# The first modulation of a two-layer latent-token backbone: half of its sixteen weight units as split products, the norm of the first half among the input tiles, the loads in another order

## The chip, the cores and the metric

One NeuronCore of a Trainium2 chip runs the whole program. The metric is device microseconds of one execution; the engines are named as in the profile: PE (TensorE), DVE (VectorE), ACT (ScalarE), POOL (GpSimd), and SP, which issues most DMAs. The time before is the median of three runs.

## The reference

Two layers over 1024 latent tokens and 256 context tokens, width 1024, all in float32. What matters here stands at the very start of layer 0:

```
def adaln(cond, w, b):
    m = jax.nn.silu(cond) @ w + b          # w: 1024 x 6144, cut in six vectors of 1024
    return jnp.split(m[..., None, :], 6, axis=-1)

sh1, sc1, g1, sh2, sc2, g2 = adaln(c, mod_w[l], mod_b[l])
n_lat = modulate(rmsnorm(h, norm1_g[l]), sh1, sc1)
csh1, csc1, ... = adaln(c_ctx, mod_w[l], mod_b[l])
n_ctx = modulate(rmsnorm(hc, norm1_g[l]), csh1, csc1)
q, k, v, xr, gr = jnp.split(n_lat @ w_in, ...)      # and n_ctx @ w_in
```

The first projection can start once the shift and scale vectors (the first 2048 columns of `mod_w[0]`) and the normed tokens are there. Attention, a gated recurrence, a short-convolution layer and two SwiGLU feed-forwards follow; the change doesn't touch them.

## The kernel before

Everything is written out by hand: each engine has one block whose instructions run in the order in which they stand, and semaphores (`wait_ge`, `then_inc`) tie the engines together. Tokens lie transposed in SBUF, features on the 128 partitions.

Large products are made of a high and a low part. A float32 operand x becomes `hi`, x rounded to the fp32r format, and `lo` = x - hi; `product` runs three fp32r matmuls, w_hi·x_hi, w_lo·x_hi and w_hi·x_lo. The rounding is a copy (ACT, or a POOL multiplication with ones), the low part a subtraction (DVE or POOL).

The prologue, which is the stretch up to the first projection:

- ACT's queue loads ten tiles `x_in` of 128 tokens (eight latent, two context; 512 KB each). SP's queue loads small parameters, then sixteen modulation units of 512 KB, `load_first_mod(u)`, into the eight places of `mod_ring`; unit u holds rows 128k to 128k+127 and 1024 columns, with c = u // 8 telling shift from scale and k = u % 8. From unit 8 on a load waits until PE has used the unit eight before. Among them stand the loads `raw` of the first projection's weights (`load_unit`; two buffers).
- PE turns each tile (eight 128x128 transposes), DVE places it in `h_in`, ACT squares and sums it. After the last tile one square root, one reciprocal and ten diagonals `x_diag` follow on ACT and DVE; `x_spread(n)` on PE spreads 1/rms over the partitions, and DVE multiplies (`x_rms`, L2363, sixteen instructions of 128x512).
- `first_mod(u)` on PE (L1191) multiplies the unit by `cond` (two columns: the latent and the context condition) as plain float32 matmuls, 2 x 512 each, adding up in banks 4 to 7. ACT and DVE copy the sums to `mod_row`, `mod_turn` (L1206) turns them, DVE adds the bias (`mods`) and makes `gains`.
- Then the norm is finished, feature tile k by tile: `scaled` (DVE L2380 for even k, ACT for odd), `act_hi` (ACT L1825), `proj_lo` (DVE L2392). PE's `columns` waits for `proj_lo` of tile k (semaphore `norm_done`) before the three matmuls of that tile, L1102 to L1104. `GROUPS` sets PE's order: unit 0 on the first half of the tokens, unit 1 on the first half, both on the second half, and so on.
- Meanwhile POOL's `split(j, ...)` makes `w_hi` (L936) and `w_lo` (L939) of the first four projection units from `raw`, into four places `w_hi4`, `w_lo4`; the two `raw` buffers come free with the semaphore `unit_split`.

## Time and profile before

| | us |
|---|---|
| median of three runs | 2296.51 (2292.99 to 2296.66) |
| the profiled execution | 2295.41 |
| its span from first to last instruction | 2293.6 |
| PE busy in the span | 2234.5 |
| first projection matmul starts | 57.77 |

The profiled execution stands 1.1 us under the median, and 1.8 us of it lie outside the span. Times of rows are microseconds from the span's start. In a row of the timeline the first number is the start, the second the time to the end of the last of the instructions merged in it, and the bracket is the idle time ahead of it with what ended it. In a row of the windows each engine has its busy time and, in brackets, its instructions; behind them stand the granted TensorE clock (1.00 is 2.4 GHz, 0.50 is 1.2 GHz), the DMA engines' busy share and GB/s.

### The profile page before, as it was taken

Reading aid. Unit: us, or ns where it says so; the run is one execution under the profiler, and the core shown is the slowest. Engines: PE = TensorE matmul, PEld = TensorE weight load, DVE = VectorE, ACT = ScalarE, POOL = GpSimd, SP = SyncE. Lnnn points to the kernel's source line nnn. Section 1 sums busy time; section 2 is a strip of 40 time slices with the busy share of each in tenths; the row PEclk is TensorE's granted clock in tenths of the full one; section 3 lists DMA queues with packets and bytes.
Section 4 is the critical chain, followed back from the end, with each engine's and each line's share of the span. In section 5 each row is a group of like instructions: output and inputs, shape, how many; then the busy total and the mean of one; then the engine's idle time right before and its main releaser. Section 6 shows DMA issues by size and latency. Waiting matters only on the chain.

```text
span 2293.6 us, 27308 instructions
## 1 busy us (share of the span) xinstructions
PE 2234.5 (97%) x10246; PEld 1819.7 (79%) x10246; DVE 1480.8 (65%) x1897; ACT 841.0 (37%) x1396; POOL 1139.1 (50%) x726
## 2 busy tenths in 40 slices
PE   7999999999999999999999899999899999999998
PEld 3788887878778888888888678888688888888886
DVE  5677765854775555558777987665975555555553
ACT  3555546852533333332213522234533333332112
POOL 3222314788545555565443445574365555564340
PEclk9999999999999999999999999999999999999999
DMA  9756558734132222247652122260132222242321
GB/s 344 211 157 172 161 170 202 166 129 138 37 110 83 83 83 83 83 169 259 219 198 96 42 83 74 74 207 10 60 98 89 83 84 83 83 153 92 110 83 74
DMA packets 296942, 282.95 MB, mean 123 GB/s; under 512 B 64783, under 2 KB 242155, under 8 KB 296299
## 3 DMA queue, kind: packets, MB, share of 16 engines
q1 hardware_dynamic: 258747, 257.61, 36.3%
q10 hardware_dynamic: 37488, 21.50, 3.3%
q8 instruction: 82, 1.34, 0.2%
q0 software_dynamic: 576, 2.10, 0.2%
q14 instruction: 49, 0.40, 0.1%
HBM read 226.36 MB, written 57.16 MB: 124 GB/s over the span
## 4 chain that ended last, share of the span: by engine, by line
PE 70%; DVE 6%; POOL 1%; issue 1%; ACT 1%; DMA 1%; DVEq 0%; POOLq 0%; ACTq 0%
PE bank L1102 23%; PE bank L1104 23%; PE bank L1103 23%; DVE act_lo L2138 1%; DVE act_hi L2138 1%; DMA pair_raw<-in_o_w_in 1%; DVE x_rms L2130 0%; PE bank L1145 0%; DVE bank L2049 0%; DVE pair_raw L2115 0%; DVE low_f L2123 0%; POOL slot L1063 0%; PE bank L1129 0%; DVE t_sum L2105 0%; DVE a L2138 0%
## 5 line engine op out<-in xcount | busy, mean ns | idle before, releaser
L2057 DVE SCALAR_TENSOR_TENSOR h<-bank,mods,h 128x512 f32<-128x512 f32 x384 | 287.2, 750 | 260.8 <-PE bank L1104 255.6
L1063 POOL TENSOR_TENSOR slot_lo<-pair_raw,slot_hi 128x512 fp32r<-128x512 f32 x112 | 170.1, 1519 | 282.1 <-ACT slot_hi L1621 282.1
L1063 POOL TENSOR_TENSOR slot_lo<-t_sum,slot_hi 128x512 fp32r<-128x512 f32 x109 | 163.6, 1523 | 158.3 <-ACT slot_hi L1621 158.3
L1063 POOL TENSOR_TENSOR slot<-pair_raw,slot 128x512 fp32r<-128x512 f32 x144 | 233.8, 1644 | 16.0 <-ACT slot L1621 16.0
L2218 DVE TENSOR_TENSOR bank<-bank,p 128x512 f32<-128x512 f32 x53 | 37.0, 698 | 290.6 <-PE bank L1104 290.6
L1102 PE MATMUL bank<-act_lo,slot_hi 128*128 128x512 f32 x436 | 170.8, 392 | 6.6 <-DVE act_lo L2138 5.9
L1621 ACT CAST slot_hi<-pair_raw 128x512 fp32r<-128x512 f32 x112 | 69.0, 616 | 287.8 <-DMA pair_raw<-in_ffn_w_gu 239.1
L1102 PE MATMUL bank<-a,slot_hi 128*128 128x512 f32 x436 | 171.5, 393 | 2.3 <-ACT p L1630 0.8
L1104 PE MATMUL bank<-a,slot_hi 128*128 128x512 f32 x436 | 170.5, 391 | 0.0
L1104 PE MATMUL bank<-act_lo,slot_hi 128*128 128x512 f32 x436 | 169.8, 389 | 0.0
L1103 PE MATMUL bank<-a,slot_lo 128*128 128x512 f32 x436 | 169.7, 389 | 0.0
L1103 PE MATMUL bank<-act_lo,slot_lo 128*128 128x512 f32 x436 | 169.7, 389 | 0.0
L1102 PE MATMUL bank<-act_hi,w_hi 128*128 128x512 f32 x368 | 146.7, 399 | 3.3 <-DVE proj_lo L2392 2.7
L1103 PE MATMUL bank<-act_hi,w_lo 128*128 128x512 f32 x376 | 147.9, 393 | 0.0
L1074 POOL TENSOR_TENSOR act_lo<-low_f,act_lo 128x512 fp32r<-128x512 f32 x80 | 102.3, 1318 | 83.8 <-ACT act_lo L1661 83.8
L1103 PE MATMUL bank<-act_hi,slot 128*128 128x512 f32 x364 | 141.9, 390 | 0.0
L1104 PE MATMUL bank<-act_hi,slot 128*128 128x512 f32 x364 | 141.8, 390 | 0.0
L1102 PE MATMUL bank<-act_hi,slot 128*128 128x512 f32 x364 | 141.7, 389 | 0.0
L1621 ACT CAST slot_hi<-t_sum 128x512 fp32r<-128x512 f32 x109 | 67.8, 622 | 165.8 <-PE bank L1104 114.3
L1102 PE MATMUL bank<-act_lo 128*128 128x512 f32 x320 | 125.8, 393 | 0.0
L1104 PE MATMUL bank<-act_lo 128*128 128x512 f32 x320 | 125.1, 391 | 0.0
L1103 PE MATMUL bank<-act_lo 128*128 128x512 f32 x320 | 124.6, 389 | 0.0
(329 smaller groups left out, 5962.2 us busy)
## 6 DMA issues: line engine op xcount, KB each, us to landing
pair_raw<-in_ffn_w_gu SPq DMA_DIRECT2D x88, 512.0 KB, 4.4
mod_in_f<-in_mod_w SPq DMA_DIRECT2D x48, 512.0 KB, 3.7
z_spill<-silu_g SPq DMA_DIRECT2D x88, 256.0 KB, 2.7
mod_in_p<-in_mod_w SPq DMA_DIRECT2D x32, 512.0 KB, 4.7
pair_raw<-in_o_w_in SPq DMA_DIRECT2D x24, 512.0 KB, 3.7
raw<-in_e_w_in SPq DMA_DIRECT2D x20, 512.0 KB, 4.5
low_f<-z_spill SPq DMA_DIRECT2D x40, 256.0 KB, 5.0
a_f<-z_spill SPq DMA_DIRECT2D x18, 512.0 KB, 6.2
```

The lines of the kernel that those rows point to most:

```text
L1063: nc.gpsimd.tensor_tensor(low, from_, high, ALU.subtract).then_inc(s_wlo, 1)
L1074: nc.gpsimd.tensor_tensor(lo, full, hi, ALU.subtract).then_inc(s_l2, 1)
L1102: pe.matmul(dst, w_hi, x_hi, start=first, stop=False)
L1103: pe.matmul(dst, w_lo, x_hi, start=False, stop=False)
L1104: return pe.matmul(dst, w_hi, x_lo, start=False, stop=last)
L1621: nc.scalar.copy(slot(st, n, p)[0], from_).then_inc(s_whi, 1)
L2057: V.scalar_tensor_tensor(out=dst, in0=bank[:, b, :], scalar=mods[:, gate, m:m + 1], in1=dst, op0=ALU.mult, op1=ALU.add).then_inc(s_hup, 1)
L2138: V.tensor_tensor(lo, LOW_F[n][k], hi, ALU.subtract).then_inc(s_ld, 1)
L2218: V.tensor_tensor(to, bank[:, x_bank(p), :], p1_at(p), ALU.add).then_inc(s_made, 1)
```

## The change

- Eight of the sixteen units (`MOD_SPLIT`: 1, 3, 5, 7, 8, 10, 12, 13) become split products. ACT makes `mod_hi(u)` (rounding the unit, 128x1024), DVE `mod_lo(u)` = unit - hi (128x1024, both inputs in SBUF), and PE runs four fp32r matmuls with a stationary of four columns, the hi and the lo part of the two conditions (`cond_s`). The other eight stay float32, with two zero columns more (`cond_d`). The four rows of the sums are folded in `mod_turn`, now a float32 matmul with a 4x2 matrix of ones (`fold_rows`) and no transpose.
- `mod_hi` and `mod_lo` use places 2 and 3 of `w_hi4` and `w_lo4`. So POOL's `split(2)` waits until all sixteen units are summed.
- PE takes the units in another order, `MOD_ORDER`: 0, 2, 1, 4, 3, 6, 5, 7, 9, 8, 11, 10, 12, 14, 13, 15; five of them among the tiles.
- Square root, reciprocal and diagonals come in three parts (first four tiles, second four, context); the first half's `x_rms` stands among the last tiles on DVE, the second half's between four `mod_low`.
- Of the `raw` loads unit 0 comes behind modulation unit 11, units 1 to 3 behind all sixteen; before, units 0 and 1 came ahead of modulation unit 8, and 2 and 3 behind units 11 and 13.
- In the first projection PE waits for `act_hi` (semaphore `normed_hi`) ahead of the first two matmuls of a tile and for `proj_lo` only ahead of the third.

```diff
+        MOD_TILE = {4: (0,), 6: (2, 1), 8: (4, 3)}
+        MOD_ORDER = tuple(u for tt in sorted(MOD_TILE) for u in MOD_TILE[tt]) + (6, 5, 7, 9, 8, 11, 10, 12, 14, 13, 15)
+        MOD_SPLIT = (1, 3, 5, 7, 8, 10, 12, 13)
+        def mod_hi(u):
+            return w_hi4[:, 2 + MOD_SPLIT.index(u) % 2, :]
...
             def load_first_mod(u):
                 if u >= 8:
-                    sp.wait_ge(s_modmm, u - 7)
+                    sp.wait_ge(*mod_done(u - 8))
...
-            for j in range(2):
-                load_unit(j, j, column_unit(w_in, order_p[j]))
             for u in range(8, 2 * FT):
                 load_first_mod(u)
-                if u in (11, 13):
-                    j = (u - 7) // 2
-                    load_unit(j, j % 2, column_unit(w_in, order_p[j]))
+                if u == 11:
+                    load_unit(0, 0, column_unit(w_in, order_p[0]))
+            for j in range(1, 4):
+                load_unit(j, j % 2, column_unit(w_in, order_p[j]))
...
             for j in range(4):
+                if j == 2:
+                    pool.wait_ge(s_modmm, 2 * FT)
                 split(j, j, j % 2)
...
                 pe.matmul(dst, w_lo, x_hi, start=False, stop=False)
+                if low_at is not None:
+                    pe.wait_ge(*low_at)
                 return pe.matmul(dst, w_hi, x_lo, start=False, stop=last)
...
+                if u in MOD_SPLIT:
+                    pe.wait_ge(s_mhi, MOD_SPLIT.index(u) + 1)
+                    pe.wait_ge(s_mlo, MOD_DVE.index(u) + 2)
+                    for a in range(2):
+                        dst, half = bank[0:4, 4 + 2 * c + a, :], slice(a * HALF, (a + 1) * HALF)
+                        pe.matmul(dst, cond_s[:, k, :], mod_hi(u)[:, half], start=first, stop=False)
+                        mm = pe.matmul(dst, cond_s[:, k, :], mod_lo(u)[:, half], start=False, stop=last)
...
-                    mm = pe.transpose(bank[:, 3, 2 * (c * FT + m):2 * (c * FT + m) + 2], mod_row[:, c, m * P:(m + 1) * P],
-                                      ident[0:2, 0:2])
+                    mm = pe.matmul(bank[:, 3, 2 * (c * FT + m):2 * (c * FT + m) + 2], mod_row[:, c, m * P:(m + 1) * P],
+                                   fold_rows[:], start=True, stop=True)
...
+            def mod_high(u):
+                n = MOD_SPLIT.index(u)
+                act.wait_ge(s_mod[u % 8], 16 * (u // 8 + 1))
+                if n >= 2:
+                    act.wait_ge(*mod_done(MOD_SPLIT[n - 2]))
+                nc.scalar.copy(mod_hi(u), mod_ring[:, u % 8, :]).then_inc(s_mhi, 1)
...
+            def mod_low(j):
+                u = MOD_DVE[j]
+                dve.wait_ge(s_mhi, MOD_SPLIT.index(u) + 1)
+                V.tensor_tensor(mod_lo(u), mod_ring[:, u % 8, :], mod_hi(u), ALU.subtract).then_inc(s_mlo, 1)
```

What the change moves on two engines, before and after. DVE, from the last context tile to the last modulation vector, before (`x_rms` is the multiplication by the spread 1/rms, `mods` the vectors with their bias):

```order
L2350 COPY ctx_t<-bank 128x8x128 [waits x_turned] x2
L2352 RECIPROCAL x_std<-x_std 128x10 [waits x_rms_ready]
L2355 TENSOR_SCALAR sp_t<-par 128x8 [waits par_placed]
L2356 TENSOR_TENSOR sp_t<-sp_t,par 128x8 [waits dve_step]
L2357 TENSOR_SCALAR half_b<-par 128x16
L2363 TENSOR_TENSOR x_rms<-h_in,bank 128x512 [waits rstd_spread,dve_step]
L2363 TENSOR_TENSOR x_rms<-h_in,bank 128x512 [waits dve_step] x7
L2363 TENSOR_TENSOR x_rms<-h_in,bank 128x512 [waits rstd_spread,dve_step]
L2363 TENSOR_TENSOR x_rms<-h_in,bank 128x512 [waits dve_step] x7
L2336 TENSOR_TENSOR mods<-bank,mod_bias 128x8 [waits mod_turned]
```

And the same place after, from the first context tile on, where the low parts of units 5, 7 and 8 are the rows that end in `mod_unit_hi` waits:

```order
L2449 COPY ctx_t<-bank 128x8x128 [waits x_turned]
L2429 TENSOR_TENSOR x_rms<-h_in,bank 128x512 [waits rstd_spread]
L2429 TENSOR_TENSOR x_rms<-h_in,bank 128x512 [waits dve_step] x3
L2449 COPY ctx_t<-bank 128x8x128 [waits dve_step,x_turned]
L2434 TENSOR_TENSOR w_lo<-mod_ring,w_hi 128x1024 [waits mod_unit_hi]
L2423 RECIPROCAL x_std<-x_std 128x2 [waits x_rms_ready]
L2434 TENSOR_TENSOR w_lo<-mod_ring,w_hi 128x1024 [waits mod_unit_hi]
L2465 TENSOR_SCALAR sp_t<-par 128x8 [waits par_placed]
L2466 TENSOR_TENSOR sp_t<-sp_t,par 128x8 [waits dve_step]
L2467 TENSOR_SCALAR half_b<-par 128x16
L2429 TENSOR_TENSOR x_rms<-h_in,bank 128x512 [waits rstd_spread,dve_step]
L2429 TENSOR_TENSOR x_rms<-h_in,bank 128x512 [waits dve_step]
```

Eight subtractions of 128x1024 have come in on DVE, two of them ahead of this piece and the last four each behind two of the second half's `x_rms`.

POOL, the four splits of the first projection's weights, before:

```order
L936 TENSOR_TENSOR w_hi<-raw,ones 128x1024 [waits raw_landed0,ident_made]
L939 TENSOR_TENSOR w_lo<-raw,w_hi 128x1024 [waits unit_hi]
L936 TENSOR_TENSOR w_hi<-raw,ones 128x1024 [waits raw_landed1]
L939 TENSOR_TENSOR w_lo<-raw,w_hi 128x1024 [waits unit_hi]
L936 TENSOR_TENSOR w_hi<-raw,ones 128x1024 [waits raw_landed0]
L939 TENSOR_TENSOR w_lo<-raw,w_hi 128x1024 [waits unit_hi]
L936 TENSOR_TENSOR w_hi<-raw,ones 128x1024 [waits raw_landed1]
L939 TENSOR_TENSOR w_lo<-raw,w_hi 128x1024 [waits unit_hi]
L952 MEMSET gate_w 128x512 [waits norm_done,h_spilled]
```

And after:

```order
L958 TENSOR_TENSOR w_hi<-raw,ones 128x1024 [waits raw_landed0,ident_made]
L961 TENSOR_TENSOR w_lo<-raw,w_hi 128x1024 [waits unit_hi]
L958 TENSOR_TENSOR w_hi<-raw,ones 128x1024 [waits raw_landed1]
L961 TENSOR_TENSOR w_lo<-raw,w_hi 128x1024 [waits unit_hi]
L958 TENSOR_TENSOR w_hi<-raw,ones 128x1024 [waits raw_landed0,mod_summed]
L961 TENSOR_TENSOR w_lo<-raw,w_hi 128x1024 [waits unit_hi]
L958 TENSOR_TENSOR w_hi<-raw,ones 128x1024 [waits raw_landed1]
L961 TENSOR_TENSOR w_lo<-raw,w_hi 128x1024 [waits unit_hi]
L976 MEMSET gate_w 128x512 [waits norm_done,h_spilled]
```

The instructions are the same; the third split now also waits for `mod_summed`, the end of PE's last modulation unit.

## Rows read from the trace of the kernel before

**Rows 1.** The page, part 1: busy time of each engine

```profile
PE 2234.5 (97%) x10246; PEld 1819.7 (79%) x10246; DVE 1480.8 (65%) x1897; ACT 841.0 (37%) x1396; POOL 1139.1 (50%) x726
```

**Rows 2.** Timeline of PE, 31 to 66 us

```profile
31.18 8.74 PE L1191 MATMUL bank<-mod_ring,cond 128*2 128x512 f32 x20
...
48.31 5.31 PE L1191 MATMUL bank<-mod_ring,cond 128*2 128x512 f32 x12
54.43 0.62 PE L1206 MATMUL bank<-ident,mod_row 2*128 2x2 f32 x8 [0.82 <-ACT mod_row L1803]
57.77 0.77 PE L1102 MATMUL bank<-act_hi,w_hi 128*128 128x512 f32 x1 [2.71 <-DVE proj_lo L2392]
...
65.34 0.39 PE L1103 MATMUL bank<-act_hi,w_lo 128*128 128x512 f32 x1
65.57 0.39 PE L1104 MATMUL bank<-proj_lo,w_hi 128*128 128x512 f32 x1
```

**Rows 3.** Windows of the prologue and the first projection

```profile
15.40:18.80 3.40, 3.30 (x4) 0.37 (x4) 0.00 (x0) 1.95 (x4) 0.00 (x0) 0.53 1.03 410
...
53.60:57.70 4.10, 0.64 (x9) 0.57 (x8) 2.85 (x8) 1.96 (x4) 0.00 (x0) 0.81 1.18 456
57.70:62.90 5.20, 5.13 (x12) 3.85 (x13) 4.46 (x8) 5.14 (x9) 0.00 (x0) 0.50 0.98 417
62.90:104.00 41.10, 41.10 (x205) 34.87 (x205) 32.75 (x61) 20.13 (x35) 11.52 (x10) 1.00 0.78 217
104.00:112.00 8.00, 7.10 (x33) 5.67 (x32) 2.25 (x3) 5.43 (x8) 2.74 (x2) 1.00 0.65 122
```

**Rows 4.** Timeline of DVE, 22 to 58 us

```profile
22.80 1.23 DVE L2350 COPY h_in<-bank 128x1024 f32<-128x1024 f32 x1 [1.60 <-PE bank L1221]
...
33.44 1.81 DVE L2356 TENSOR_TENSOR sp_t<-sp_t,par 128x8 f32<-128x8 f32 x1
...
41.13 11.52 DVE L2363 TENSOR_TENSOR x_rms<-h_in,bank 128x512 f32<-128x512 f32 x16 [5.79 <-PE bank L1197]
...
53.66 0.68 DVE L2367 COPY mod_row<-bank 2x512 f32<-2x512 f32 x1 [0.73 <-PE bank L1191]
...
55.37 0.17 DVE L2082 SCALAR_TENSOR_TENSOR gains<-mods,par 128x8 f32<-128x8 f32 x1
...
55.65 1.00 DVE L2380 TENSOR_SCALAR scaled<-x_rms,gains,mods 128x512 f32<-128x512 f32 x2
56.93 0.69 DVE L2392 TENSOR_TENSOR proj_lo<-scaled,act_hi 128x512 fp32r<-128x512 f32 x1 [0.28 <-ACT act_hi L1825]
```

**Rows 5.** Timeline of POOL, 33 to 48 us

```profile
33.34 1.90 POOL L936 TENSOR_TENSOR w_hi<-raw,ones 128x1024 fp32r<-128x1024 f32 x1
...
45.37 2.35 POOL L939 TENSOR_TENSOR w_lo<-raw,w_hi 128x1024 fp32r<-128x1024 f32 x1
```

**Rows 6.** Timeline of DVE, 86 to 111 us

```profile
86.79 2.50 DVE L2437 SCALAR_TENSOR_TENSOR x_conv<-x_pad,par,x_conv 128x256 f32<-128x256 f32 x1
89.22 3.42 DVE L2437 SCALAR_TENSOR_TENSOR x_conv<-x_pad,par,x_conv 128x1024 f32<-128x1024 f32 x1
...
109.35 1.22 DVE L2487 TENSOR_TENSOR xc_lo<-x_conv,xc_hi 128x1024 fp32r<-128x1024 f32 x1
```

**Rows 7.** Timeline of POOL, 86 to 92 us

```profile
86.54 2.48 POOL L939 TENSOR_TENSOR w_lo<-raw,w_hi 128x1024 fp32r<-128x1024 f32 x1 [1.77 <-ACT w_hi L1857]
88.97 2.59 POOL L939 TENSOR_TENSOR w_lo<-raw,w_hi 128x1024 fp32r<-128x1024 f32 x1
```

**Rows 8.** Timeline of ACT, 85 to 88 us

```profile
85.41 2.00 ACT L1857 CAST w_hi<-raw 128x1024 fp32r<-128x1024 f32 x2
```

**Rows 9.** The matmuls of line L1145, 290 to 1100 us (min/median/max ns)

```profile
L1145 PE MATMUL bank<-ones,mod_acc_p x16: 165/250/250, 342.2 to 343.8; 128*128 128x1 f32 x16
```

**Rows 10.** Waits of SP's queue, first 200 us: total, times, longest

```profile
SPq L658 <- POOL gate_w L952: 7.3, 1, 7.3
```

**Rows 11.** Window of the first 48 us

```profile
0.00:48.00 48.00, 39.46 (x161) 17.22 (x162) 21.86 (x26) 20.12 (x40) 18.99 (x22) 0.96 0.95 342
```

More of the change, by code:

```diff
@@ L922, in _ @@
             nc.gpsimd.memset(ones[:], 1.0).then_inc(s_ident, 1)
+            steps.run(nc.gpsimd.memset(cond_d[:, :, 2:4], 0.0))
+            nc.gpsimd.tensor_tensor(fold_rows[:], ident[0:4, 0:2], ident[0:4, 2:4], ALU.add).then_inc(s_ident, 1)
             nc.gpsimd.memset(far_rows[:], FAR).then_inc(s_far, 1)
@@ L1098, in _, with product @@
         def _(pe):
-            def product(dst, w, x_hi, x_lo, first, last):
+            def product(dst, w, x_hi, x_lo, first, last, low_at=None):
                 w_hi, w_lo = w
@@ L1188, in first_mod @@
                 c, k = divmod(u, FT)
-                pe.wait_ge(s_mod[u % 8], 16 * (u // 8 + 1))
-                for a in range(2):
-                    mm = pe.matmul(bank[0:2, 4 + 2 * c + a, :], cond[:, k, :], mod_ring[:, u % 8, a * HALF:(a + 1) * HALF],
-                                   start=(k == 0), stop=(k == FT - 1))
+                nth = sum(v // FT == c for v in MOD_ORDER[:MOD_ORDER.index(u)])
+                first, last = nth == 0, nth == FT - 1
+                if u in MOD_SPLIT:
[5 more added lines that the diff above has]
+                        mm = pe.matmul(dst, cond_s[:, k, :], mod_lo(u)[:, half], start=False, stop=last)
+                else:
+                    pe.wait_ge(s_mod[u % 8], 16 * (u // 8 + 1))
+                    for a in range(2):
+                        mm = pe.matmul(bank[0:4, 4 + 2 * c + a, :], cond_d[:, k, :], mod_ring[:, u % 8, a * HALF:(a + 1) * HALF],
+                                       start=first, stop=last)
                 mm.then_inc(s_modmm, 1)
             def x_spread(n):
+                pe.wait_ge(s_rstd, n + 1)
                 for j in range(NORMS[n][2] // P):
@@ L1780, in _, with x_root, x_diagonals, mod_rows @@
             nc.scalar.activation(x_std[:, 1, 0:1], zero[:, 0:1], ACT.Silu).then_inc(s_xsq, 1)
+            def x_root(n):
+                lo, hi = tiles_of(n)
+                act.wait_ge(s_xsq, hi + 1)
+                nc.scalar.activation(x_std[:, 1, lo:hi], x_std[:, 0, lo:hi], ACT.Sqrt, bias=eps_t[:, 0:1], scale=1.0 / D).then_inc(s_xstd, 1)
+            def x_diagonals(n):
+                lo, hi = tiles_of(n)
+                act.wait_ge(s_xinv, n + 1)
+                act.wait_ge(s_turn, 2)
+                for j in range(lo, hi):
+                    last = nc.scalar.activation(x_diag[:, j, :], ident[:], ACT.Copy, scale=x_std[:, 2, j:j + 1])
+                last.then_inc(s_rstd, 1)
+            def mod_high(u):
[4 more added lines that the diff above has]
+                nc.scalar.copy(mod_hi(u), mod_ring[:, u % 8, :]).then_inc(s_mhi, 1)
+            def mod_rows(c):
+                act.wait_ge(s_modmm, FT * (c + 1))
+                for a in range(2 - c):
+                    nc.scalar.copy(mod_row[:, c, a * HALF:(a + 1) * HALF], bank[0:4, 4 + 2 * c + a, :]).then_inc(s_modrow, 1)
+            HIGH_AT = {5: (1,), 7: (3,), 9: (5, 7)}
             for tt in range(TT + CT):
@@ L2339, in _, with x_inverse, x_normed @@
                 dve.sem_inc(s, credits)
+            def x_inverse(n):
+                lo, hi = tiles_of(n)
+                dve.wait_ge(s_xstd, n + 1)
+                V.reciprocal(x_std[:, 2, lo:hi], x_std[:, 1, lo:hi]).then_inc(s_xinv, 1)
+            def x_normed(n, fs):
+                dve.wait_ge(s_bc, n + 1)
+                for f in fs:
+                    src, _, w, *_ = NORMS[n]
+                    steps.run(V.tensor_tensor(x_rms[:, f, cols(n)], src[:, f, cols(n)], bank[:, SPREAD[n], 0:w], ALU.mult))
+            def mod_low(j):
+                u = MOD_DVE[j]
+                dve.wait_ge(s_mhi, MOD_SPLIT.index(u) + 1)
+                V.tensor_tensor(mod_lo(u), mod_ring[:, u % 8, :], mod_hi(u), ALU.subtract).then_inc(s_mlo, 1)
+            LOW_AT = {6: 0, 7: 1}
             for tt in range(TT + CT):
+                if tt == 5:
+                    x_inverse(0)
+                if tt == TT:
+                    x_inverse(1)
                 if tt == 4:
@@ L2357, in _ @@
             steps.run(V.tensor_scalar(half_b[:], par[:, PAR["br"]:PAR["br"] + 16], 0.5, None, ALU.mult))
-            for n in (0, 1):
-                dve.wait_ge(s_bc, n + 1)
-                for f in range(FT):
-                    src, _, w, *_ = NORMS[n]
-                    steps.run(V.tensor_tensor(x_rms[:, f, cols(n)], src[:, f, cols(n)], bank[:, SPREAD[n], 0:w], ALU.mult))
-                if n == 1:
-                    mod_first(0)
+            for q in range(4):
+                x_normed(1, range(2 * q, 2 * q + 2))
+                mod_low(4 + q)
+            mod_first(0)
             dve.wait_ge(s_modmm, 2 * FT)
-            V.tensor_copy(mod_row[:, 1, HALF:UNIT], bank[0:2, 7, :]).then_inc(s_modrow_d, 1)
+            V.tensor_copy(mod_row[:, 1, HALF:UNIT], bank[0:4, 7, :]).then_inc(s_modrow_d, 1)
             mod_first(1)
```

110 lines of the change are left out of this document (74 added, 36 removed).

## The prediction

> **What bounds the kernel now.** The page's busy times come first: PE works in 97% of the span [rows 1], so whatever moves the start of its dense part moves the end. The timeline of PE then shows where the dense part starts: modulation units without a pause from 31.18 to 39.9 and, behind the spreads, three more units from 48.31 to 53.62, the turn of the last sums from 54.43, and the first projection matmul at 57.77, which waited 2.71 us for `proj_lo` [rows 2]. The windows show what follows: 41.10 of 41.10 us busy from 62.9 to 104, and 0.90 us idle in the next 8 [rows 3]. So nothing behind the prologue has slack worth naming, and I carry a shift of the first projection to the end one to one. The same windows show the clock: 0.53 in 15.4 to 18.8 and 0.50 in 57.7 to 62.9, each behind a gap of PE, and 1.00 from 62.9 on [rows 3].
>
> I take two marks. T is the end of the last modulation unit, 53.6. H is the end of unit 0 on the first half of the tokens, 65.8: the last of its 24 matmuls starts at 65.57 and they follow each other by 0.23 [rows 2]. H - T is 12.2.
>
> **PE's own work.** A float32 unit takes 1.77 us (three in 5.31), a split one four matmuls at 0.23, 0.92 [rows 2]. Eight times 0.85 is 6.8 us less for PE. If PE were all that counts, T would be 46.8. The turn becomes eight float32 matmuls instead of eight transposes: at most the 1.7 us of the sixteen records of L1145 [rows 9], at least the 0.62 of the transposes [rows 2]; I take 1.3, near the former, since the form is the same (eight float32 matmuls with few columns). Its second use stands behind T.
>
> **DVE's work.** It gets eight subtractions of 128x1024 with both inputs in SBUF. The same form took 1.22 us for `xc_lo` [rows 6]: 9.8 us. ACT's eight roundings at 1.0 [rows 8] are lighter, but its queue stops once: the diagonals of tiles 4 to 7 wait for a reciprocal that DVE makes only behind four `x_rms`, at about 32, so unit 5 is rounded at 35.5 and unit 7 at 37.
>
> I follow the queues. Unit 0 is unchanged and cold (to 18.8 [rows 3]). Tile 5, the first spread and tile 6 bring PE to 21.9; DVE places tile 6 (1.23 [rows 4]) until 23.1 and makes low 1 until 24.4; PE has unit 1 until 25.3 and tile 7 until 26.4; DVE places it until 27.6. From there DVE has seven subtractions (8.5), sixteen `x_rms` (11.52 [rows 4]), two placements (2.5) and small things (0.9): 23.4 us in one queue, so 51.0 without a single wait. PE meanwhile is through with unit 6 at 32.9, and needs low 5, which stands behind eight `x_rms` and both context placements and ends at 38.5 at best. That is an idle of 5.6 us or more, and as behind the gaps of [rows 3] I expect the clock at 0.50 behind it, for some 5 us: units 5 and 7 and the second spread at half speed. The second half's `x_rms` wait for that spread, which costs DVE 1 to 2 us.
>
> **What POOL does to DVE.** This is the term on which the sign hangs. When POOL ran `w_lo` from 86.54 to 89.02, DVE's 128x256 operation issued at 86.79 ended at 89.29, and the 128x1024 one behind it took 3.42, until 1.1 us after POOL's second `w_lo` ended at 91.56 [rows 6, 7]. At 33.44 even an operation on 128x8 took 1.81, until POOL's `w_hi` ended at 35.24 [rows 4, 5]. Against that, sixteen `x_rms` (one input in SBUF, one in PSUM) took 0.72 each [rows 4] though POOL worked until 47.7 [rows 5]. So I read: DVE operations that take all from SBUF and POOL's take turns, each waiting for the whole of the other; those with an input in PSUM don't. All eight `mod_low`, `gains`, `scaled` and `proj_lo` are of the first kind. The Trainium skill, page "SBUF — State Buffer", section "Who interferes with whom", says the same: a VectorE instruction with two SBUF inputs, or in a two-port mode, fully blocks against a GpSimd one that reads SBUF. By that rule the sum is the one below; by a reading without it, it would be +0.5 to +4.3 (the first rival). The page speaks against this change.
>
> The loads put the clashes in place. The DMA engines moved 342 GB/s over the first 48 us at 0.95 busy [rows 11]. `raw` of unit 0 is now the 23rd piece of 0.524 MB, 12.1 MB, so it lands at 35 to 36. POOL splits it in two pieces of 1.90 and 2.35 [rows 5], just when DVE comes to low 5 and low 7: low 5 waits 0.9, low 7 2.2. Units 13 to 15 wait for PE's units 5 to 7 and `raw` 1 stands behind them, landing at 48 to 50; its split costs low 12 and low 13 another 0.5 to 2.7. Together: 51.0, plus 1 to 2 for the spread, plus 3.5 to 4.5, is about 56; unit 13 (0.9) and unit 15 (1.8) behind the last low part give **T = 58.8**, between 57.7 and 60.2. That is +5.2, although PE has 6.8 us less to do.
>
> **Behind T.** Before: POOL was idle from 47.7 [rows 5], `gains` at 55.37, `scaled` at 55.65, the first `proj_lo` from 56.93 to 57.62 [rows 4], that is T + 4.0. Now `split(2)` and `split(3)` start at T: 1.90, 2.35, 1.90, 2.35, together 8.5. DVE's `mod_row` copy and `mods` read PSUM and pass; two `gains` and the first `scaled` get one turn each between POOL's pieces, and they lengthen POOL's row by 0.7. The first `proj_lo` ends at about T + 10.1, 6.1 later than before, whether the turn takes 0.7 or 1.3. The changed wait lets PE start with the high part some 0.9 us ahead of that, which before would have been worth 0.85; now it only fills time for which PE is late anyway. From there `proj_lo` comes at 0.95 per tile as before, and PE ends unit 0 at T + 18.2: **H - T = 18.2 instead of 12.2, +6.0**. Bounds: +3.5 if POOL starts late enough that one of its pieces falls behind the first `scaled`, +8 if the first `scaled` loses a further turn.
>
> **At no cost.** The loads of units 4 and 5 and the sixteen bias fills on SP's queue, which now wait for `split(2)` and `split(3)`; behind them stand the gate weights, for which SP waited 7.3 us for POOL's memset anyway [rows 10], and that memset follows `norm_done`, so moves by the same shift. The gate matmuls are 45 us further. If the fills were not through, gates would be late by one to three us. The spilling of `h_in` goes with T.
>
> **Sum.** 5.2 + 6.0 = 11.2 on the profiled execution's 2295.4 is 2306.6; with the median 1.1 above it the same sum gives 2307.7. I forecast **2307**.
>
> **Rivals.**
> - *No turns between POOL and DVE for these forms.* For it: `x_rms` was untouched [rows 4], and no row shows a subtraction of 128x1024 caught. Then T is 54.1 with PE warm behind its gap and 57.9 with the clock at 0.50, and H - T stays at 12.2: +0.5 to +4.3, so 2296 to 2300. 11 in 100, mostly inside the bound of no change.
> - *Part of the clashes.* POOL's splits of units 0 and 1 fall beside DVE's `x_rms`, and only those behind T count, or the other way: +5 to +8.5, 2300.5 to 2304. 15 in 100.
> - *Faster.* DVE is not in PE's way: `mod_low` and `x_rms` run at less than the 1.22 and 0.72 of the rows, or the early part of PE's queue is not held by low 5. It decides if DVE's 23.4 us shrink below 15: then PE's 6.8 and the 0.85 of the wait come through, less 0.7 for the turn: 2288.5. Against it stand two rows of [rows 4, 6]. 6 in 100.
> - *More than the forecast.* PE stays at clock 0.50 through units 9 to 15, since it starts and stops: four float32 units at 3.4 instead of 1.77 add 6.5, less the slack of 3 us in which it waits: +15 and more, 2311 to 2316. 8 in 100.
> - The forecast itself, +9 to +14: 60 in 100.
>
> **Range and chances.** 2299 to 2313 takes the forecast, the partly paid case and the cold edge, and leaves the faster case, most of the first rival and the far cold end outside. About 0.2%, 4.6 us, is what a measurement of this kernel can tell from no change. Faster 0.06, the same 0.10, slower 0.84.
>
> **What the changed profile would show.** PE idle for 5 us or more ahead of the split unit 5, which waits for DVE. The clock under 1.00 in the windows of 38 to 45. Subtractions of 128x1024 on DVE with a mean near 1.7 us where single ones take 1.2. T at 58 to 60. Behind T four POOL operations in a row, `gains` and the first `scaled` each ending when one of POOL's ends, and the first projection matmul at T + 8 to T + 10. From 80 us on the same rows as before, shifted. I am wrong if low parts take 1.2 beside POOL, or if T lies below 53, or if the shift of the first projection does not reach the end.

## The result and the profile after

| | before | after |
|---|---|---|
| median | 2295.8 us (2292.99 to 2296.66, 6 runs) | 2310.49 us (2307.62 to 2311.86, 6 runs) |
| profiled execution | 2295.41 | 2311.86 |
| its span | 2293.6 | 2310.1 |

The ratio is 1.006, with an interval from 1.0049 to 1.007, which is 11 to 16 us; by the medians the changed kernel is 14.7 us slower. The forecast was 2307, from 2299 to 2313.

PE's busy time has hardly moved from 2234.5 [rows 1]:

```profile
PE 2237.3 (97%) x10262; PEld 1828.3 (79%) x10262; DVE 1491.8 (65%) x1908; ACT 849.3 (37%) x1408; POOL 1140.5 (49%) x728
```

The timeline of PE, which answers to [rows 2]: the start, the time to the end, and in brackets the idle time ahead of the row with what ended it.

```profile
30.89 1.88 PE L1228 MATMUL bank<-mod_ring,cond_d 128*4 128x512 f32 x4
39.17 0.58 PE L1223 MATMUL bank<-w_hi,cond_s 128*4 128x512 f32 x1 [6.41 <-DVE w_lo L2434]
39.56 0.63 PE L1224 MATMUL bank<-w_lo,cond_s 128*4 128x512 f32 x1
...
49.90 1.94 PE L1244 MATMUL bank<-fold_rows,mod_row 4*128 4x2 f32 x16
...
56.17 1.88 PE L1228 MATMUL bank<-mod_ring,cond_d 128*4 128x512 f32 x4
58.87 1.91 PE L1244 MATMUL bank<-fold_rows,mod_row 4*128 4x2 f32 x16 [0.82 <-ACT mod_row L1846]
65.43 0.77 PE L1126 MATMUL bank<-act_hi,w_hi 128*128 128x512 f32 x1 [4.65 <-ACT act_hi L1903]
67.74 0.80 PE L1130 MATMUL bank<-proj_lo,w_hi 128*128 128x512 f32 x1 [1.12 <-DVE proj_lo L2499]
...
74.30 0.39 PE L1130 MATMUL bank<-proj_lo,w_hi 128*128 128x512 f32 x1
```

PE has unit 6 done at 32.8 and stands for 6.41 us until DVE's low part of unit 5 is there. From 39.17 on it has no pause until the last modulation unit ends, T = 58.05, which is 4.4 later than before. The turn takes 1.91 where the transposes took 0.62 [rows 2]. The first projection matmul waits for `act_hi` and starts at 65.43, 7.7 later than before, and unit 0 on the first half, whose last matmul starts at 74.30, ends at H = 74.5, 8.7 later. So H - T is 16.5, where it was 12.2.

DVE's timeline, which answers to [rows 4]:

```profile
36.89 2.14 DVE L2434 TENSOR_TENSOR w_lo<-mod_ring,w_hi 128x1024 fp32r<-128x1024 f32 x1
38.95 0.15 DVE L2423 RECIPROCAL x_std<-x_std 128x2 f32<-128x2 f32 x1
39.03 3.31 DVE L2434 TENSOR_TENSOR w_lo<-mod_ring,w_hi 128x1024 fp32r<-128x1024 f32 x1
...
44.30 1.23 DVE L2434 TENSOR_TENSOR w_lo<-mod_ring,w_hi 128x1024 fp32r<-128x1024 f32 x1
...
61.09 1.37 DVE L2160 SCALAR_TENSOR_TENSOR gains<-mods,par 128x8 f32<-128x8 f32 x1
...
62.58 4.51 DVE L2487 TENSOR_SCALAR scaled<-x_rms,gains,mods 128x512 f32<-128x512 f32 x2
67.01 1.28 DVE L2499 TENSOR_TENSOR proj_lo<-scaled,act_hi 128x512 fp32r<-128x512 f32 x2
```

And POOL's, which answers to [rows 5]:

```profile
36.05 1.89 POOL L958 TENSOR_TENSOR w_hi<-raw,ones 128x1024 fp32r<-128x1024 f32 x1 [22.11 <-DMA raw<-in_e_w_in]
38.03 3.23 POOL L961 TENSOR_TENSOR w_lo<-raw,w_hi 128x1024 fp32r<-128x1024 f32 x1
50.07 2.37 POOL L958 TENSOR_TENSOR w_hi<-raw,ones 128x1024 fp32r<-128x1024 f32 x1 [8.81 <-DMA raw<-in_e_w_in]
...
58.13 1.89 POOL L958 TENSOR_TENSOR w_hi<-raw,ones 128x1024 fp32r<-128x1024 f32 x1 [2.40 <-PE bank L1228]
60.10 2.34 POOL L961 TENSOR_TENSOR w_lo<-raw,w_hi 128x1024 fp32r<-128x1024 f32 x1
62.40 1.90 POOL L958 TENSOR_TENSOR w_hi<-raw,ones 128x1024 fp32r<-128x1024 f32 x1
64.37 2.43 POOL L961 TENSOR_TENSOR w_lo<-raw,w_hi 128x1024 fp32r<-128x1024 f32 x1
```

The two are to be laid side by side. Low 5 ends at 39.03, 1.1 behind the end of POOL's `w_hi` at 37.94; low 7 ends at 42.34, 1.1 behind the end of `w_lo` at 41.26; where POOL is idle a low part takes 1.23. `gains`, eight columns wide, ends at 62.46, as POOL's piece ends at 62.44. Two `scaled`, which took 1.00 together before [rows 4], take 4.51: each stands for one POOL piece.

The windows, which answer to [rows 3]:

```profile
34.00:46.00 12.00, 6.83 (x20) 3.03 (x20) 11.53 (x14) 5.49 (x10) 5.12 (x2) 0.72 0.52 164
...
66.00:70.00 4.00, 2.88 (x7) 1.83 (x6) 3.96 (x6) 3.47 (x7) 0.80 (x1) 0.50 0.91 278
84.00:118.00 34.00, 34.00 (x174) 29.06 (x174) 20.84 (x40) 10.45 (x20) 12.40 (x11) 1.00 0.73 173
118.00:130.00 12.00, 8.70 (x37) 6.45 (x36) 3.75 (x4) 11.41 (x18) 5.24 (x3) 0.86 0.27 63
```

Behind the pause of 6.41 the granted clock is at its lower level for a while (0.72 over 34 to 46). The first projection is dense again (34.00 of 34.00 us busy), and the gates that follow it, idle for 0.90 of 8 us before [rows 3], now leave PE 3.3 of 12 us.

That is not all. Take each matmul's start, matched from the last matmul backwards, and subtract the start of the same matmul before: the difference is the **shift**, and it shows where the profiled execution loses what. The columns are places, in microseconds of the kernel before:

```
 66 (H)   104    130    340    400    455    500   1290   1400    end
  8.7     8.7   11.2   12.3   13.5   13.9   15.2   15.2   16.3   16.5
```

Only 8.7 of the 16.5 us arise in the prologue. The other 7.7 come later: 2.5 at the gates, 1.1 until 340, 1.1 around 372, where attention loads `k_lo`, 1.3 around 464, and 1.1 around 1350. The two profiled executions do not stand at their medians: of the 16.5, 1.8 are theirs (2311.86 is 1.4 above its median, 2295.41 is 0.4 below). The kernel before, run 70 times more on three chips, took from 2293.1 to 2299.7, so a single step of 1 to 2 us in such a row need not belong to the kernel.

### The profile page after: what moved, and what is told of

It reads as the page before. It is cut to its first block, busy times and chain, and to the rows that moved or that the text cites. A ratio compares the mean times of both kernels' runs of the same rounds, so it can differ in the third digit from the quotient of the medians.

```text
span 2310.1 us, 27370 instructions
## 1 busy us (share of the span) xinstructions
PE 2237.3 (97%) x10262; PEld 1828.3 (79%) x10262; DVE 1491.8 (65%) x1908; ACT 849.3 (37%) x1408; POOL 1140.5 (49%) x728
## 4 chain that ended last, share of the span: by engine, by line
PE 71%; DVE 5%; issue 1%; ACT 1%; POOL 1%; DMA 0%; DVEq 0%; POOLq 0%; ACTq 0%
PE bank L1126 23%; PE bank L1130 23%; PE bank L1127 23%; DVE act_lo L2216 1%; DVE act_hi L2216 1%; DVE x_rms L2208 0%; PE bank L1172 0%; DVE bank L2127 0%; DVE low_f L2201 0%; DVE pair_raw L2193 0%; PE bank L1156 0%; DVE a L2216 0%; PE bank L1374 0%; DVE x_rms L2210 0%; PE bank L1195 0%
```

## Experiments

Each run is given with its median against that of the kernel before on the same chip (2296.4, 2296.6 and 2296.8 in the three groups), its T and H - T, and later its shifts in one table. The ratio with its interval is not exactly the quotient of the two medians; the difference in us is that of the medians.

**POOL's late splits alone** (in the kernel before):

```diff
             for j in range(4):
+                if j == 2:
+                    pool.wait_ge(s_modmm, 2 * FT)
                 split(j, j, j % 2)
```

> The kernel before, with one line of the change: POOL's third and fourth split wait until all sixteen modulation units are summed. Everything else, the loads too, stays as before. If POOL and DVE take turns, the four POOL operations (8.5 us) run from T = 53.6 to 62 beside gains, scaled and proj_lo: the first scaled pair ends 3 to 5 us later, the first projection matmul moves from 57.8 to 62 or 64, unit 0 on the first half ends 4 to 6 us later, and the end comes 4 to 8 us later. If they don't take turns, nothing on PE moves and the time is within 1 us of before.

Measured: 2302.09, ratio 1.0023 (1.0014 to 1.0032), +5.7. T is 52.2, H 69.0: H - T is 16.9 instead of 12.2, as much as the changed kernel shows behind T (16.5). T itself lies 1.4 earlier than before; that is the clock at unit 0, told at the run on the turn. DVE's timeline:

```profile
54.29 4.60 DVE L2382 TENSOR_SCALAR scaled<-x_rms,gains,mods 128x512 f32<-128x512 f32 x2
58.81 3.43 DVE L2394 TENSOR_TENSOR proj_lo<-scaled,act_hi 128x512 fp32r<-128x512 f32 x2
```

POOL's four pieces start at 52.27 and end at 61.08. So one added wait, with nothing else changed, costs 4.7 us on the path.

**The split wait alone** (in the kernel before):

```diff
                 pe.matmul(dst, w_lo, x_hi, start=False, stop=False)
+                if low_at is not None:
+                    pe.wait_ge(*low_at)
                 return pe.matmul(dst, w_hi, x_lo, start=False, stop=last)
...
-                        pe.wait_ge(s_norm, 8 * norm + k + 1)
+                        pe.wait_ge(s_nhi, 8 * norm + k + 1)
...
```

> The kernel before, with the split wait alone: in the first projection PE waits for act_hi ahead of the first two matmuls of a tile and for proj_lo ahead of the third. I expect the first projection matmul at 57.0 instead of 57.8 and the end 0.5 to 0.9 us earlier, which the timing can hardly tell from nothing. The rival: PE only starts and stops more often, at clock 0.50 for longer, and nothing or up to 2 us is lost.

Measured: 2300.59, ratio 1.0011 (1.0003 to 1.002), +4.2. PE begins the projection 0.7 earlier and ends unit 0 0.4 earlier, as expected; and still the kernel is slower, by more than the rival's 2 us if one takes the medians (the ratio's interval is 0.7 to 4.6 us). In the profiled execution the shift says where: 0.4 at 340 and 4.9 at 400. PE's timeline there:

```profile
375.52 0.80 PE L1315 MATMUL bank<-k_hi,q_st 128*128 128x512 f32 x1 [3.85 <-DMA k_lo<-k_spill]
376.12 0.63 PE L1316 MATMUL bank<-k_lo,q_st 128*128 128x512 f32 x1
```

The same two matmuls in the kernel before:

```profile
372.54 0.50 PE L1312 MATMUL bank<-k_hi,q_st 128*128 128x512 f32 x1 [1.41 <-DMA k_lo<-k_spill]
372.88 0.40 PE L1313 MATMUL bank<-k_lo,q_st 128*128 128x512 f32 x1
```

The data came 3.0 later, though nothing that makes `k_lo` was touched: SP issued the load 0.9 later (363.54 against 362.64), and it took 11.9 us to land instead of 9.9. Behind the longer pause the matmuls run at half the clock (0.63 for 0.40). This execution, at 2302.59, was the slowest of the kernel's twelve; two others took 2295.35 and 2296.16, no more than the kernel before. So the loss at `k_lo` is shown for one execution, and the same kernel may do without it.

**The splits held until both halves are normed** (in the changed kernel):

```diff
                 if j == 2:
                     pool.wait_ge(s_modmm, 2 * FT)
+                    pool.wait_ge(s_norm, 2 * FT)
```

> The changed kernel, with POOL's third split waiting further, until DVE has finished the norms of both halves (norm_done 16), so that no POOL operation runs beside gains, scaled and proj_lo. If the turns cost what the trace after shows behind T (16.5 from T to the end of unit 0 on the first half, against 12.2), the stretch falls back to 11.5 to 12.5 and the end comes 4 to 5 us earlier than with the change, near 2306. The rival: the later splits of units 2 and 3 and the loads, bias fills and gate weights behind them on SP's queue come too late, and PE waits ahead of its sixth group or ahead of the gates; then the gain is eaten, 2310 or more.

Measured: 2315.18, ratio 1.0079 (1.0067 to 1.0091), +18.8. The local gain is there: T 57.3, H 70.0, so H - T is 12.7 instead of 16.5. It is more than lost further on. What waits for the late splits is late (the loads of units 4 and 5, the bias fills, the gate weights, for which ACT waited 3.13), and at the gates the shift goes from 5.4 to 16.1. This is what the rival had said. ACT and PE there:

```profile
123.82 1.04 ACT L1936 CAST w_hi<-raw 128x1024 fp32r<-128x1024 f32 x1 [6.95 <-DMA raw<-in_e_w_in]
```

```profile
128.62 0.58 PE L1127 MATMUL bank<-xc_hi,gate_hi 128*128 128x256 f32 x1 [6.74 <-ACT lru_r L1987]
```

**No split units** (in the changed kernel; norm among the tiles, order of units, order of loads, float32 turn and split wait stay):

```diff
-        MOD_SPLIT = (1, 3, 5, 7, 8, 10, 12, 13)
+        MOD_SPLIT = ()
...
-                if j == 2:
-                    pool.wait_ge(s_modmm, 2 * FT)
                 split(j, j, j % 2)
...
```

> The changed kernel without its split products: all sixteen units float32 with four columns, no rounding on ACT, no subtraction on DVE, no waiting of POOL for the sums; the order of units, the norm of the first half among the tiles, the order of the loads and the turn as matmuls stay. If the eight subtractions and their place behind x_rms on DVE are what keeps T at 58, T comes back to 52.5 to 54.5 and the end to 2293 to 2297. The rival: the order of DVE (x_rms ahead of the context tiles, late raw loads) is to blame by itself, and T stays at 56 or more.

Measured: 2300.82, ratio 1.0018 (1.001 to 1.0027), +4.4. PE:

```profile
47.87 7.03 PE L1226 MATMUL bank<-mod_ring,cond_d 128*4 128x512 f32 x16
...
59.62 0.77 PE L1124 MATMUL bank<-act_hi,w_hi 128*128 128x512 f32 x1 [1.99 <-ACT act_hi L1900]
```

T is 54.9, 3.1 earlier than with the eight split units, and H - T 12.7. The parts that save PE work cost 3.1 us ahead of T and, by their wait on POOL, 3.8 behind it. T and the time lie somewhat above what was expected (54.5, and 2297 at most); the rival, T at 56 or more, is out.

**DVE's queue in another order** (in the changed kernel):

```diff
-            LOW_AT = {6: 0, 7: 1}
+            LOW_AT = {6: 0, 7: 1, 8: 2, 9: 3}
...
-                if tt == TT:
+                if tt == TT - 1:
                     x_inverse(1)
+                    x_normed(0, range(0, 2))
...
+            x_normed(0, range(2, FT))
+            dve.sem_inc(s_xr, 1)
+            mod_low(4)
...
```

> The changed kernel with DVE's queue in another order: the reciprocal of tiles 4 to 7 and two x_rms ahead of the placement of tile 7, the low parts of units 5 and 7 right behind the context placements, the other six x_rms of the first half behind them. Nothing is left out. Theory (PE's idle of 6.41 us ahead of unit 5 is the order's, since ACT's rounding stood 7.46 us behind a reciprocal that DVE made late): unit 5 follows unit 6 within 1 us, PE waits 2 to 4 us ahead of unit 9 instead, the last unit ends at 52 to 54 instead of 58.05, the rest as in the changed kernel: 2304.5 to 2307. Rival (DVE's total of low parts and x_rms, 23 us in one queue, sets the end whatever the order): the last unit ends at 57 or later, 2309 to 2311.

Measured: 2307.72, ratio 1.0045 (1.0031 to 1.0059), +11.1. The time lies between the two claims. The pause ahead of unit 5 is gone (it starts at 32.06 instead of 39.17), but T is 59.2, 1.1 later than in the changed kernel, where the rival had it (57 or later). PE's timeline:

```profile
45.22 0.39 PE L1223 MATMUL bank<-w_hi,cond_s 128*4 128x512 f32 x1 [3.39 <-DVE w_lo L2434]
...
46.48 3.57 PE L1244 MATMUL bank<-fold_rows,mod_row 4*128 4x2 f32 x16
```

and DVE's:

```profile
38.29 2.34 DVE L2463 TENSOR_SCALAR sp_t<-par 128x8 f32<-128x8 f32 x1
...
42.40 2.67 DVE L2434 TENSOR_TENSOR w_lo<-mod_ring,w_hi 128x1024 fp32r<-128x1024 f32 x1
```

The early units brought the load of `raw` for unit 1 forward, POOL's second split began at 42.10 instead of 50.07, and it fell on low 10. An operation on 128x8 took 2.34, until POOL's `w_lo` ended at 40.60. From 45.9, behind the pause of 3.39, PE was at half clock until 56, the first turn among it with 3.57.

**The same with POOL silent up to T:**

```diff
-                if j == 2:
+                if j == 0:
                     pool.wait_ge(s_modmm, 2 * FT)
```

> The kernel with DVE's queue in the other order (a_order), and POOL holds all four splits of the first projection's weights, not only the third and fourth, until the last modulation unit is summed. Nothing is left out; behind that unit it must be slow, only the prologue up to there is looked at. Theory (in a_order POOL's splits of units 0 and 1 took turns with low 10, low 12 and a constant, 1.4 + 0.7 + 2.2 us, and the pause before low 10 put the granted clock at 0.50 for the next ten us): all low parts take 1.22, PE has no pause over 3 us, the last modulation unit ends at 52 to 54.5 instead of 59.1. Rival (DVE's total sets the end): 57 or later with low parts at 1.22. The time: 2312 to 2320.

Measured, in a single execution: 2307.8, less than the 2312 to 2320 expected. DVE's low 10, and PE's last unit:

```profile
39.17 1.22 DVE L2434 TENSOR_TENSOR w_lo<-mod_ring,w_hi 128x1024 fp32r<-128x1024 f32 x1
```

```profile
49.61 1.88 PE L1228 MATMUL bank<-mod_ring,cond_d 128*4 128x512 f32 x4
```

Every low part takes 1.22 to 1.23 and T is 51.5: 7.7 earlier, and 2.1 earlier than in the kernel before. Not all of it is POOL's silence: unit 0 took 1.88 here and 3.39 in the run before this one, and unit 9 started 1.05 earlier (36.07 against 37.12) although no low part had met POOL by then. Of the 2.1 against the kernel before, where unit 0 took 3.41, some 1 is left by the same estimate. So the split units cost nothing, and seem to gain a little, if DVE is left alone and its queue is in a fitting order. What POOL still had to do then came behind T (H - T 17.6), and the shift grew to 9.8 by the gates.

**The form of the turn** (in the kernel before):

```diff
-                    mm = pe.transpose(bank[:, 3, ...], mod_row[:, c, m * P:(m + 1) * P], ident[0:2, 0:2])
+                    mm = pe.matmul(bank[:, 3, ...], mod_row[:, c, m * P:(m + 1) * P], ident[0:2, 0:2], start=True, stop=True)
```

> The kernel before with the turn of the modulation rows as eight float32 matmuls by a 2x2 identity instead of eight transposes. Nothing is left out. Theory (the turn's form costs 1.3 us each time, 1.9 instead of 0.62, and both stand on PE's path): turn 1.9 us, the first projection 2.6 us later than 57.77 if the first turn is on the path too, 1.3 if it hides in PE's waits: 2297.7 to 2299. Rival (it is the four rows, not the form): turn below 1 us, no change in the prologue, and what differs in time is from later phases.

Measured: 2301.2, ratio 1.002 (1.0011 to 1.003), +4.6.

```profile
53.58 1.91 PE L1206 MATMUL bank<-ident,mod_row 2*128 2x2 f32 x16 [0.82 <-ACT mod_row L1803]
```

With two rows it takes 1.91 too: it is the form (sixteen records for eight instructions), not the four rows. H comes 0.9 later. T was 52.8 here, 0.9 earlier than before although the first turn was 1.3 longer. The trace shows why: unit 0 started 0.6 earlier (14.88) and took 1.88 where it had taken 3.41. This is the kernel before, and under it the run with POOL's late splits, whose program is the same up to there:

```profile
15.50 3.41 PE L1191 MATMUL bank<-mod_ring,cond 128*2 128x512 f32 x4 [2.79 <-DMA mod_ring<-in_mod_w]
```

```profile
15.59 1.88 PE L1193 MATMUL bank<-mod_ring,cond 128*2 128x512 f32 x4 [2.80 <-DMA mod_ring<-in_mod_w]
```

The pauses are equal and the clock behind them is not. The four matmuls of unit 0 took 1.88 in four of the fourteen profiled executions and 2.30 to 3.57 in the others, behind pauses of 2.4 to 2.8, and that difference of the clock moves T and H by some 1.5 us with no change in the program. So where T or H of two kernels differ by less than 1.5 us, one execution of each doesn't tell them apart; H - T is free of what happens at unit 0. The rest of the 4.6 comes later.

**A version meant to keep the gain.** Units 1, 3, 5 and 7 alone are split; POOL, idle then, makes the low parts; they lie in places of input tiles that are through, so `split(2)` waits for nothing; two `raw` loads and two `x_rms` stand earlier; the turn is a transpose of four rows:

```diff
+        mod_h = [at(40, "mod_h0", [P, UNIT], F32R), at(48, "mod_h1", [P, UNIT], F32R)]
+        mod_l = [at(44, "mod_l0", [P, UNIT], F32R), at(52, "mod_l1", [P, UNIT], F32R)]
...
+            for n, u in enumerate(MOD_SPLIT):
+                pool.wait_ge(s_mhi, n + 1)
+                nc.gpsimd.tensor_tensor(mod_lo(u), mod_ring[:, u % 8, :], mod_hi(u), ALU.subtract).then_inc(s_mlo, 1)
             for j in range(4):
-                if j == 2:
-                    pool.wait_ge(s_modmm, 2 * FT)
                 split(j, j, j % 2)
...
```

> A version meant to keep what the split units give and to drop what they cost: only units 1, 3, 5 and 7 are split, their low parts are made by POOL (idle until raw lands) and not by DVE, high and low parts lie in places of input tiles that are through, so that POOL's third split waits for nothing and raw of units 0 and 1 are loaded behind modulation units 10 and 12; the turn is a transpose of four rows again and DVE adds the pairs. Nothing is left out. Theory: PE has no idle behind unit 6, 4 x 0.85 us less than with sixteen float32 units, so the last unit ends at 51 to 52, and the end of unit 0 on the first half follows by 12.3 (POOL's splits are through): at 63.5 to 64.5, 1.3 to 2.3 us earlier than before; if nothing is lost later, 2294 to 2295. Rival 1 (POOL's splits reach beyond the last modulation unit, so DVE takes turns with them again): the distance is 15 us or more, 2298 or later. Rival 2 (later phases lose 2 to 4 us in any kernel whose prologue moves, as in the four runs so far): 2297 to 2299.

Measured: 2297.89 (2297.02 to 2300.57), ratio 1.0006 (0.9997 to 1.0015): no difference from the kernel before, as the second rival had it (2297 to 2299). PE's timeline:

```profile
43.80 7.03 PE L1232 MATMUL bank<-mod_ring,cond_d 128*4 128x512 f32 x16
51.65 0.62 PE L1248 MATMUL bank<-ident,mod_row 4*128 4x4 f32 x8 [0.82 <-ACT mod_row L1851]
54.66 0.77 PE L1130 MATMUL bank<-act_hi,w_hi 128*128 128x512 f32 x1 [2.38 <-ACT act_hi L1904]
```

The prologue is what it was to be, and better: T 50.8, H 62.7, both about 3 us earlier than before, with unit 0 as slow as there (3.46 against 3.41). Its profiled execution, 2.7 above its own median, was 5.2 later at the end: 2.4 were lost until 340 and 4.9 around the load of `k_lo`.

**Only a later start.** POOL clears a buffer four times or twice ahead of every load, and nothing else changes:

```diff
+            for _ in range(4):
+                steps.run(nc.gpsimd.memset(raw[:, :, :], 0.0))
+            pool.sem_inc(s_go, 2)
...
+            sp.wait_ge(s_go, 1)
...
+            act.wait_ge(s_go, 1)
```

Four times, in the kernel before:

> The kernel before with nothing changed but a start that is some 8 to 12 us late: POOL clears a buffer four times before the first load of any queue is issued. Nothing is left out. Theory 1 (what is lost behind the prologue in the changed kernels, 6 to 8 us in the profiled runs, comes from the order of events, above all from loads and buffers that move against PE): here all moves together, the shift of PE against before is the same at 60, 372, 465, 1303 and at the end within 0.7 us, and the time is 2296.4 plus the delay. Theory 2 (the granted clock falls behind the same short gaps of PE at some times of the execution and not at others): the shift grows by 1.5 to 3 us at 465 or 1303 with a granted clock under 1.00 there, though nothing moved against anything.

Twice, in the kernel before, in the changed kernel and in the last version:

> The kernel before with POOL clearing the buffer twice ahead of all loads: the start is 3.7 us late and nothing else changed. With four clearings the start was 7.5 us late and the median rose by 9.2. Theory 1 (the kernel before stands at a favourable place, and any other place loses 1 to 3 us behind the prologue, at 372, 465, 620 and 1350): 3.7 + 1 to 3, 2301 to 2303.5. Theory 2 (what is lost grows with the delay): 3.7 + 0.8, 2301. Theory 3 (chance of the runs): anything between 2298 and 2305, not the same as either.

> The changed kernel with POOL clearing the buffer twice ahead of all loads, 3.7 us late. If the loss behind the prologue (some 5.5 us of the changed kernel's 14) belongs to its order of events, it stays: 2313.5 to 2315. If it depends on where in time the later pauses fall, it can shrink or grow: 2311 to 2317, and the shift of PE against the changed kernel is not 3.7 throughout.

> The version with four split units and low parts on POOL (a_best: the first projection 3.2 us earlier than before, the end 1.3 us later by the medians), 3.7 us late by two clearings. Its prologue then ends 0.5 us behind that of the kernel before. If what it lost later (8 us in the profiled run) is the price of arriving earlier, against loads that don't come earlier, the shift at 372 us is the same as there and the time is 2298 to 2299. If the loss belongs to the version itself, it is 2301 to 2302.

| | start of PE later by | median against before | ratio |
|---|---|---|---|
| before, four clearings | 7.5 | +9.2 (2305.82) | 1.0038 (1.0025 to 1.005) |
| before, two | 3.6 | +5.4 (2302.18) | 1.0022 (1.0013 to 1.0031) |
| the changed kernel, two | 3.4 | +14.7 (2311.51) | 1.0062 (1.005 to 1.0075) |
| the last version, two | 3.6 | +4.9 (2301.66) | 1.0022 (1.0013 to 1.0031) |

By the medians either delay of the kernel before loses 1.7 to 1.8 more than itself, which is what the first theory said; but the intervals (6 to 11 us and 3.0 to 7.1 us) contain the bare delays of 7.5 and 3.6, so that the extra is not shown. The changed kernel with two clearings has the ratio of the changed kernel without (1.006), and its median is 1.0 higher (2311.51 against 2310.49): most of the 3.4 us at the start do not come out at the end, though the intervals leave room for about 3 us either way. The last version lost the 3.6 (2301.66 against 2297.89), which fits a loss that is its own and not only the price of an earlier arrival.

The shifts of all profiled executions against the kernel before, at the same places as above:

```
                         66(H)   104   130   340   400   455   500  1290  1400   end
changed kernel             8.7   8.7  11.2  12.3  13.5  13.9  15.2  15.2  16.3  16.5
POOL's late splits         3.2   3.2   3.0   3.5   3.5   5.8   5.9   5.8   5.5   5.5
split wait                -0.4  -0.4  -0.1   0.4   4.9   4.9   6.4   6.6   7.2   7.1
held until normed          4.2   5.4  16.1  17.3  19.1  19.5  20.8  20.8  20.0  20.2
no split units             1.8   1.8   3.1   3.2   3.5   3.6   4.9   4.9   5.2   5.3
DVE's other order         10.2  10.2  11.1  12.0  12.7  13.1  14.3  14.2  14.6  14.8
... and POOL silent        3.3   6.1   9.8  10.2  10.6  11.1  12.4  12.4  12.2  12.4
float32 turn               0.9   0.9   0.5   1.4   3.5   3.5   4.8   4.8   6.1   6.1
last version              -3.1  -3.1  -1.6  -0.7   4.2   4.2   4.4   4.1   5.2   5.2
before, 7.5 later          7.9   7.9   8.5   8.6   8.4   8.4   8.5   8.3   9.4   9.4
before, 3.6 later          4.6   4.6   5.0   5.1   5.6   5.7   6.8   6.8   7.1   7.1
changed, 3.4 later        12.6  12.6  14.4  14.8  14.9  15.3  16.4  16.4  16.0  16.1
last version, 3.6 later    0.2   0.2   1.5   1.7   4.5   4.5   6.2   6.0   6.3   6.3
```

Two things stand out in the medians and the columns. Every kernel's median is above what its own prologue (the column H) gave, by 0.8 to 6.0 us, and by 14.6 in the kernel held until both halves are normed; so something is lost behind the prologue in all of them. At which places it is lost is seen in one execution of each only. Between 340 and 400 the kernels that come to the load of `k_lo` at +1.7 or less lose 2.1 to 4.9, those that come later -0.2 to 1.8; the kernel before, at 0, waited 1.41 and kept its clock. And between 455 and 500 all but three lose 1.1 to 1.7. There the windows of 6.7 us from the same matmul on, behind a pause of 2.3 us in each, read in the kernel before, with two and with four clearings:

```profile
463.30:470.00 6.70, 6.59 (x42) 5.60 (x43) 5.66 (x12) 6.29 (x13) 5.68 (x4) 1.00 0.01 4
```

```profile
469.00:475.70 6.70, 6.66 (x37) 6.05 (x38) 4.76 (x11) 5.12 (x11) 5.71 (x4) 0.78 0.01 3
```

```profile
471.70:478.40 6.70, 6.59 (x42) 5.60 (x43) 5.66 (x12) 6.28 (x13) 5.69 (x4) 1.00 0.04 14
```

But for the clearings the program is the same, the pause is the same, and the granted clock is 1.00, 0.78 and 1.00, with 42, 37 and 42 matmuls in the window.

## Why the prediction was right, and where it was not

**The term on which the sign hung: right, and shown.** DVE operations that take all from SBUF and POOL's take turns. Low 5 and low 7 were to wait 0.9 and 2.2 and waited 0.9 and 2.1. The eight low parts took 13.0 instead of 9.8, so 3.2 in turns, where the prediction took 3.5 to 4.5 (its own terms add up to 3.6 to 5.8). The runs with and without POOL (42.40 2.67 against 39.17 1.22) settle it. The first rival, no turns, is out. The section of the Trainium skill named in the prediction (page "SBUF — State Buffer", section "Who interferes with whom") also lists `tensor_scalar` among the operations that can enter a two-port mode and then contend; the trace agrees: two `scaled` (TENSOR_SCALAR) took 4.51 beside POOL and 1.00 without.

**PE idle ahead of unit 5, then cold: right.** 5.6 or more was 6.41, and the half clock, put at some 5 us, lasted from 39.2 to about 44.

**What sets T: the step failed, its size survived.** I said that DVE's queue reaches 56 and two units follow. DVE's last low part ended at 53.5, since only one of the last two stood for POOL, and for 0.25 us; PE was the one without a pause from 39.17 to 58.05. What I had left out of PE's queue stands there: the first turn with 1.94 and the half clock on units 5, 7 and the second spread. T came 4.4 later, not 5.2. That the two are near is luck in part: the first turn stood in no sum of T, and the clock at unit 0 alone moves T by some 1.5.

**POOL's turns behind T: right, by 4.3 instead of 6.0.** POOL's row of four, `gains` and `scaled` came as told, and the first `proj_lo` ended at 67.7, T + 9.6 (T + 10.1 told). The step that failed is that the split wait "only fills time for which PE is late anyway". The two matmuls of the high part ran at 65.43, ahead of that `proj_lo`, and two `proj_lo` then came together (1.28), so that PE had 6.8 us from there to H instead of 8.2. The price of the added wait itself is shown twice: 4.7 in the kernel before, 3.8 in the changed one.

**The turn: mis-sized.** It takes 1.9 instead of the 1.3 taken. The first turn stands on PE's path; the second does not with its whole length, since `gains`, issued at 61.09, stood for POOL's piece until 62.44 in any case. The bound of 1.7 was too low even for [rows 9]: from the first of the sixteen starts to the end of the last it is 1.84, with one column instead of two.

**"At no cost": right in the changed kernel, with a small margin.** The bias fills were issued by 83.84, POOL's memset came at 87.99 and the gate weights at 88.55, 9.0 later than before (79.52), with PE 8.7 later. SP still waited 4.7 us for the memset, where it had waited 7.3. Holding the third split until 77.7 instead of 58.1 used the margin up and cost 10.7 at the gates. The 2.5 that the changed kernel itself loses there come another way. ACT's `qk_hi`, before and after, in the group ahead of the gates:

```profile
99.44 0.60 ACT L1879 ACTIVATE qk_hi<-bank 128x512 fp32r<-128x512 f32 x1 [7.73 <-DMA q_spill<-qk_raw]
```

```profile
109.67 0.60 ACT L1957 ACTIVATE qk_hi<-bank 128x512 fp32r<-128x512 f32 x1 [9.23 <-DMA q_spill<-qk_raw]
```

It stood 1.5 longer until a spill of `q` had landed, so it came 10.2 later where PE was 8.7 later, and the gate matmuls started 10.7 later (121.39 against 110.67). Without split units ACT stood 8.71 at the same place, and the gates lost 1.3. Why the transfer landed later stays open.

**One to one to the end: wrong.** The prologue gave 8.7 and the end 16.5 in the profile, 14.7 by the medians. Had I sized the prologue right, I would have said about 2304.5. The forecast of 2307 came near by luck: its prologue was 2.5 too large while 6 us behind it were missing. The step that failed is "nothing behind the prologue has slack worth naming", from which the shift was carried on one to one. Every variant lost something behind the prologue, also those without split units. That the kernel before stands at a favourable place is one reading: in its profiled execution it waits 1.4 for `k_lo` where its nearest variants wait up to 3.9, and behind the pause at 463 its clock stays up. It rests on one execution of each kernel, and the kernel before has slower executions too, up to 2299.7: of its 70 on three chips those with a mean granted clock of 0.996 or 0.997 have medians of 2295.3 and 2294.3, those with 0.994 one of 2298.5. What makes `k_lo` late, and what decides whether the clock falls behind equal pauses, stays open.

## What to carry to other kernels

Work that is taken off the busiest engine and given to another has to be laid against every partner of that other engine: here 6.8 us less for PE were eight operations of 1.22 to 3.31 more for DVE, which takes turns with POOL, and PE stood. Before a wait is added to a queue that is off the path, ask who runs beside it at the new time: POOL's four pieces cost nothing up to 47.7 and 4.7 us when they began at T. And in a kernel that is dense to 97% a gain of 3 us in the prologue is not a gain until the end shows it: later pauses and loads cost as much more or less from one kernel to the next, and from one execution of a kernel to the next. One profile of each kernel doesn't tell the two apart.
